# Dense expert gates: one-hot matrices and matmuls, or indirect accumulating transfers through DRAM

## The chip, the cores and the metric

The kernel runs on one core of a Trainium2 chip. The metric is the device time of one launch in microseconds, as the median of several runs. The kernel before takes 1502.28 us (three runs, 1501.57 to 1502.87).

## What is computed

Two transformer blocks on 256 tokens of width 1024, in float32. The part that the change touches is the expert layer of the first block, with 16,384 experts. Cut to what matters:

```python
q = (xb @ w_query).reshape(t, 8, 2, 128)                 # 8 heads, two half queries each
scores = einsum("thpc,hpkc->thpk", q, sub_keys)          # against 128 keys for each half
s1, i1 = top_k(scores[:, :, 0], 16);  s2, i2 = top_k(scores[:, :, 1], 16)
cand = s1[..., :, None] + s2[..., None, :]               # 256 candidates per token and head
top_s, top_pos = top_k(cand, 16)
idx = take_along_axis(i1[..., :, None] * 128 + i2[..., None, :], top_pos)
gate = softmax(top_s)
act = gelu(einsum("td,thkd->thk", xb, expert_down[idx]))
out = einsum("thk,thkd->td", gate * act, expert_up[idx])
```

So each token uses 8 x 16 experts, the gates of an expert that several heads choose add up, and all other gates are zero. The kernel computes it densely: all 16,384 hidden values of every token, times a dense gate matrix that is zero but for 128 entries per token, times all of `expert_up`.

## The kernel before

All weights stream from DRAM as 412 tiles of 128x1024 values, two to a transfer of 1 MB. SyncE issues these transfers into `raw`, two halves of two tiles (lines 286 to 292). To keep float32 precision each tile is split: ScalarE copies it to `whi` (line 331), VectorE subtracts to get `wlo` (line 344), and TensorE makes three products for each 128x128 block, high by high, low by high and high by low (lines 348 to 350), 24 matmuls a tile. `whi` and `wlo` are rings of four; a split for tile u waits until tile u - 4 is used (`w_used`), and the engines prepare three tiles ahead (`LEAD`). Order on every engine is written out by hand, with semaphores between engines.

The tiles come in stages: 20 of the first projection (`W_PROJ1`), 8 of the output, 16 of the query (`W_QUERY`), 128 of `expert_down` (`W_EXP`, the hidden tiles), 128 of `expert_up` (`W_UP`, the up projection), then the second block. In the hidden stage each tile gives 128 experts by 256 tokens, ScalarE writes their gelu to a row of `ea` (lines 1101 and 1105). In the up projection ScalarE and VectorE split each row of `ea` into `phi` and `plo` (lines 1141 and 1560), and `add_outer` adds its products to PSUM.

The selection runs on VectorE beside the first 60 hidden tiles. `top16` finds the best 16 of 32 sets of 128 scores, then of 16 sets of 256 candidates, for all heads at once; after every 8 or 4 instructions `next_tile` puts in the `wlo` of one weight tile. ScalarE takes one exponential (line 1112). VectorE compares candidate positions with a count (line 1468), GpSimd multiplies the comparison by the key numbers (line 312), VectorE sums (line 1482). TensorE transposes keys and gates (line 754).

The dense gates are built from hidden tile 64 on. For a group of four tokens VectorE writes one-hot matrices of the second key (`one_hots`, line 1492) and of the first key (line 1493), the latter times the gate in three bfloat16 parts (line 1499); TensorE multiplies them, 12 matmuls a group (`gate_group`, line 762), and VectorE multiplies the result into `ea` (`apply_gates`, line 1507). One group follows each weight tile: the 64 groups of the first half of the experts beside hidden tiles 64 to 127, those of the second half beside the first 64 tiles of the up projection.

## Time and profile before

| | |
|---|---|
| median of three runs | 1502.28 us |
| span of the profiled execution | 1499.1 us |
| TensorE busy | 1423.8 us, 95% |
| VectorE busy | 1107.4 us, 74% |
| ScalarE busy | 689.6 us, 46% |
| GpSimd busy | 25.0 us, 2% |
| moved by DMA | 223.04 MB, mean 149 GB/s |

Busy times say which engine could be the bound; matmuls are pipelined, so TensorE's busy time is no sum of costs. The chain that ended last is followed back from the end of the run and tells which instructions set the time. "L762" is line 762 of the kernel. An idle time is put down to the instruction that released it.

### The profile page before, as it was taken

Reading aid. Unit: us, or ns where it says so; the run is one execution under the profiler, and the core shown is the slowest. Engines: PE = TensorE matmul, PEld = TensorE weight load, DVE = VectorE, ACT = ScalarE, POOL = GpSimd, SP = SyncE. Lnnn points to the kernel's source line nnn. Section 1 sums busy time; section 2 is a strip of 40 time slices with the busy share of each in tenths; the row PEclk is TensorE's granted clock in tenths of the full one; section 3 lists DMA queues with packets and bytes.
Section 4 is the critical chain, followed back from the end, with each engine's and each line's share of the span. In section 5 each row is a group of like instructions: output and inputs, shape, how many; then the busy total and the mean of one; then the engine's idle time right before and its main releaser. Section 6 shows DMA issues by size and latency. Waiting matters only on the chain.

```text
span 1499.1 us, 32502 instructions
## 1 busy us (share of the span) xinstructions
PE 1423.8 (95%) x12164; PEld 1392.5 (93%) x12164; DVE 1107.4 (74%) x1975; ACT 689.6 (46%) x1012; POOL 25.0 (2%) x15
## 2 busy tenths in 40 slices
PE   6999999999699999999999999999998998999986
PEld 6998899999699999999999999999988897999986
DVE  6775737999968888888899996555576667666665
ACT  5823456667453333333333334444454444444434
POOL 0000000000500000000000000000000000000000
PEclk9999999999899999999999999999999998999998
DMA  5320344455254334443444434555554224555532
GB/s 214 127 99 1 143 169 145 166 194 181 99 197 141 140 140 140 142 146 135 143 147 148 147 140 147 189 175 189 176 194 153 101 97 157 172 195 173 193 113 85
DMA packets 31311, 223.04 MB, mean 149 GB/s; under 512 B 3553, under 2 KB 3681, under 8 KB 4497
## 3 DMA queue, kind: packets, MB, share of 16 engines
q1 hardware_dynamic: 30528, 218.22, 41.3%
q0 software_dynamic: 720, 3.97, 0.8%
q8 instruction: 42, 0.69, 0.2%
q14 instruction: 21, 0.16, 0.0%
HBM read 221.13 MB, written 1.05 MB: 148 GB/s over the span
## 4 chain that ended last, share of the span: by engine, by line
PE 82%; DVE 10%; issue 3%; ACT 3%; DMA 2%; ACTq 0%; DVEq 0%; SPq 0%
PE ps L348 24%; PE ps L349 23%; PE ps L350 23%; PE ps L762 6%; DVE wlo L344 3%; DMA raw<-in_wts 1%; ACT whi L331 1%; DVE h L491 1%; PE ps L456 1%; DVE i L1441 1%; DVE sc L1438 1%; DVE sq L428 1%; PE ps L704 0%; PE ps L623 0%; DVE alo L512 0%
## 5 line engine op out<-in xcount | busy, mean ns | idle before, releaser
L344 DVE TENSOR_TENSOR wlo<-raw,whi 128x1024 fp32r<-128x1024 f32 x412 | 502.2, 1222 | 168.8 <-ACT whi L331 164.6
L331 ACT ACTIVATE whi<-raw 128x1024 fp32r<-128x1024 f32 x412 | 435.2, 1058 | 403.9 <-PE ps L350 354.9
L348 PE MATMUL ps<-ahi,whi 128*128 128x256 f32 x2016 | 586.0, 291 | 28.3 <-DVE wlo L344 12.7
L349 PE MATMUL ps<-alo,whi 128*128 128x256 f32 x2016 | 574.0, 285 | 0.0
L350 PE MATMUL ps<-ahi,wlo 128*128 128x256 f32 x2016 | 573.5, 284 | 0.0
L348 PEld LDWEIGHTS ps<-ahi,whi 128*128 128x128 f32 x2016 | 391.4, 194 | 36.2 <-issue 27.1
L349 PEld LDWEIGHTS ps<-alo,whi 128*128 128x128 f32 x2016 | 390.6, 194 | 0.3 <-issue 0.2
L350 PEld LDWEIGHTS ps<-ahi,wlo 128*128 128x128 f32 x2016 | 390.2, 194 | 0.0
L348 PE MATMUL ps<-phi,whi 128*128 128x256 f32 x1200 | 342.7, 286 | 1.6 <-DVE plo L1560 1.6
L349 PE MATMUL ps<-plo,whi 128*128 128x256 f32 x1200 | 339.0, 282 | 0.0
L350 PE MATMUL ps<-phi,wlo 128*128 128x256 f32 x1200 | 338.3, 282 | 0.0
L348 PEld LDWEIGHTS ps<-phi,whi 128*128 128x128 f32 x1200 | 228.4, 190 | 2.2 <-DVE plo L1560 2.0
L350 PEld LDWEIGHTS ps<-phi,wlo 128*128 128x128 f32 x1200 | 225.7, 188 | 0.0
L349 PEld LDWEIGHTS ps<-plo,whi 128*128 128x128 f32 x1200 | 225.3, 188 | 0.0
L1560 DVE TENSOR_TENSOR plo<-ea,phi 128x256 fp32r<-128x256 f32 x128 | 54.5, 426 | 100.3 <-ACT phi L1141 98.0
L1105 ACT ACTIVATE ea<-ps 128x256 f32 x120 | 46.2, 385 | 175.7 <-PE ps L350 175.6
L762 PE MATMUL ps<-oh,oh 128*128 128x64 bf16 x1536 | 116.5, 241 | 0.0
L762 PEld LDWEIGHTS ps<-oh,oh 128*128 128x128 bf16 x1536 | 93.9, 119 | 5.6
L1507 DVE TENSOR_TENSOR ea<-ea,ps 128x256 f32 (+1 forms) x128 | 95.9, 750 | 0.0
L1499 DVE TENSOR_TENSOR oh<-oheq,gT 128x768 bf16<-128x768 bf16 x128 | 71.5, 559 | 14.4
L1492 DVE TENSOR_TENSOR oh<-iota,kT 128x512 bf16<-128x512 bf16 x128 | 53.6, 418 | 3.9 <-PE ps L762 3.9
L1141 ACT ACTIVATE phi<-ea 128x256 fp32r x124 | 49.6, 400 | 2.2 <-DVE ea L1507 2.2
(321 smaller groups left out, 963.0 us busy)
## 6 DMA issues: line engine op xcount, KB each, us to landing
raw<-in_wts SPq DMA_DIRECT2D x206, 1024.0 KB, 4.8
cst<-in_c POOLq DMA_DIRECT2D x1, 1216.0 KB, 12.6
x<-in_x_t SPq DMA_DIRECT2D x1, 1024.0 KB, 5.0
kk<-in_keys POOLq DMA_DIRECT2D x1, 1024.0 KB, 5.1
out_dram<-h SPq DMA_DIRECT2D x4, 256.0 KB, 2.5
cs<-in_c POOLq DMA_DIRECT2D x1, 960.0 KB, 5.1
wp<-in_w_pool POOLq DMA_DIRECT2D x1, 256.0 KB, 13.0
pt<-in_ple_t POOLq DMA_DIRECT2D x1, 256.0 KB, 5.8
```

The costliest lines, as they stand in the source:

```text
L331: nc.scalar.activation(whi[:, j, :], raw_tile(j // 2, j % 2), ACT.Copy).then_inc(s["w_hi"], 1)
L344: nc.vector.tensor_tensor(wlo[:, j, :], raw_tile(j // 2, j % 2), whi[:, j, :].bitcast(F32), ALU.subtract).then_inc(s["w_lo"], 1)
L348: nc.tensor.matmul(out_ap, wh, xh, start=first, stop=False, skip_group_check=True)
L349: nc.tensor.matmul(out_ap, wh, xl, start=False, stop=False, skip_group_check=True)
L350: return nc.tensor.matmul(out_ap, wl, xh, start=False, stop=last, skip_group_check=True)
L762: m = tm(bank(2 + j, half, base=t * half), oh2[:, j, :, t], oh1[:, j, part, :, t], start=part == 0, stop=part == 2)
L1105: A(row_of(quad * 4 + (base + n)), bank(n % 2, T), ACT.Gelu).then_inc(s["gelu"], 1)
L1141: A(phi[:, n % 2, :], row_of(quad * 4 + (base + n)), ACT.Copy).then_inc(s["p_hi"], 1)
L1492: V.tensor_tensor(oh2[:, j, :, :], iota[:, :, :], m3(v[1], P), ALU.is_equal)
L1499: V.tensor_tensor(oh1[:, j, :, :, :], oheq[:, j, :, :].unsqueeze(1).to_broadcast([P, 3, half, GT]), v.unsqueeze(2).to_broadcast([P, 3, hal ...
L1507: V.tensor_tensor(v, v, bank(2 + j, GT * half).rearrange("p (t e) -> p t e", t=GT), ALU.mult)\
L1560: V.tensor_tensor(plo[:, r, :], src, phi[:, r, :].bitcast(F32), ALU.subtract).then_inc(s["p_split"], 1)
```

## The change

The dense gates are no longer computed by matmul. A DRAM scratch `gates_dense` with one float for each expert and token (16.8 MB) is zeroed by four transfers from GpSimd's queue during the first projection. VectorE selects head by head, beginning in the query stage, and writes for each head and each of 16 choices the place of its gate in the scratch (`spot`) and the gate. `spend` counts booked microseconds and puts in a weight tile's `wlo` each 1.5. ScalarE takes the exponential of each head ahead of the hidden tiles listed in `EXP_AT`. GpSimd multiplies nothing; for each head it issues 32 indirect transfers that add 128 gates each, one per partition, to the scratch, with a wait for all earlier ones between heads. When all have landed it reads the scratch back, four tiles to a transfer, into two buffers `gd`, and in the up projection VectorE multiplies each row of `ea` by its tile of `gd`, two tiles ahead, before ScalarE makes `phi`. `gate_group`, the one-hots, the transposes of keys and gates and `apply_gates` are gone, and the up projection is one loop over 128 tiles.

```diff
+BEAT = 1.5
+EXP_AT = (0, 8, 20, 32, 44, 56, 68, 80)
...
+        dense = nc.dram_tensor("gates_dense", (N_EXP * P * T, 1), F32).ap()
...
+            blank = pf[:, :, :].rearrange("p a t -> p (a t)")
+            nc.gpsimd.memset(blank, 0.0).then_inc(s["zero_ok"], 1)
+            pl.wait_ge(s["zero_ok"], 1)
+            rows_ = dense.rearrange("(p a b) o -> p a (b o)", p=P, b=2 * T)
+            n_rows = rows_.shape[1] // 4
+            for part in range(4):
+                pl.wait_ge(s["evac"], 4 * part + 2)
+                pl.dma_start(rows_[:, part * n_rows:(part + 1) * n_rows, :], m3(blank, n_rows)).then_inc(s["zeroed"], 16)
...
-            for half_, e in ((0, eq0), (1, eq1)):
-                pl.wait_ge(s["key_eq"], half_ + 1)
-                nc.gpsimd.tensor_tensor(e[:, :, :, :], e[:, :, :, :],
-                                        i16s[:, :, half_, :].unsqueeze(2).to_broadcast([P, TB * NH, TOPK, TOPK]),
-                                        ALU.mult).then_inc(s["key_mul"], 1)
...
+            pl.wait_ge(s["zeroed"], 64)
+            for h in range(NH):
+
+                pl.wait_ge(s["pick"], h + 1)
+                if h:
+                    pl.wait_ge(s["scat"], 16 * TB * TOPK * h)
+                for tb in range(TB):
+                    for k in range(TOPK):
+                        pl.indirect_dma_start(
+                            out=dense, out_offset=bass.IndirectOffsetOnAxis(ap=spot[:, tb, h, k:k + 1], axis=0),
+                            in_=gate[:, tb, h, k:k + 1], in_offset=None, compute_op=ALU.add).then_inc(s["scat"], 16)
+            pl.wait_ge(s["scat"], 16 * TB * TOPK * NH)
+            by_tile = dense.rearrange("(n p t) o -> p n (t o)", p=P, t=T)
+            for quad in range(N_EXP // 4):
+                if quad >= 2:
+                    pl.wait_ge(s["g_mul"], 4 * (quad - 1))
+                pl.dma_start(gd[:, quad % 2, :, :], by_tile[:, 4 * quad:4 * quad + 4, :])\
+                  .then_inc((s["gd0"], s["gd1"])[quad % 2], 16)
...
-            def gate_group(j):
-                for t in range(GT):
-                    for part in range(3):
-                        m = tm(bank(2 + j, half, base=t * half), oh2[:, j, :, t], oh1[:, j, part, :, t],
-                               start=part == 0, stop=part == 2)
-                m.then_inc(s["g_ps"], 1)
...
+            with pe.Fori(0, N_EXP // 4) as i:
                 for n in range(4):
                     pe.wait_ge(s["w_lo"], i * 4 + (W_UP + n + 1))
                     pe.wait_ge(s["p_split"], i * 4 + (n + 1))
                     add_outer(n, phi[:, n % 2, :], plo[:, n % 2, :])
...
+            def p_hi(n, quad=None):
+                if quad is None:
+                    act.wait_ge(s["g_mul"], n + 1)
...
+            for h in range(NH):
+
+                act.wait_ge(s["cv_ready"], h + 1)
+                A(cv[:, h % 2, :, :], cv[:, h % 2, :, :], ACT.Exp).then_inc(s["cv_exp"], 1)
+                until = EXP_AT[h + 1] if h + 1 < NH else N_EXP - 4
+                if until > EXP_AT[h]:
+                    with act.Fori(EXP_AT[h] // 4, until // 4) as i:
+                        for n in range(4):
+                            gelu(n, i)
+            for n in range(N_EXP - 4, N_EXP):
+                gelu(n)
+                if n == N_EXP - 3:
+                    p_hi(0)
...
+            def spend(us):
+
+                spent[0] += us
+                if spent[0] >= BEAT:
+                    spent[0] -= BEAT
+                    next_tile()
...
+            def candidates(h):
+
+                dve.wait_ge(s["scores"], 2 * h + 2)
+                top16(lambda k: v16[:, k[0], k[1], :], lambda k: i16[:, k[0], k[1], :],
+                      lambda k: sc[:, k[0], 2 * h + k[1], :], [(tb, c) for tb in range(TB) for c in range(2)], 0.28)
+                ch(V.tensor_tensor(cand4, over_k(v16[:, :, 0, :]), over_j(v16[:, :, 1, :]), ALU.add))
...
+            def choose(h):
+
+                best = cv[:, h % 2, :, :]
+                top16(lambda tb: best[:, tb, :], lambda tb: ci[:, tb, :], lambda tb: cand[:, tb, :], [0, 1], 0.42)
+                ch(V.tensor_copy(gsum[:, 0, :], best[:, :, 0]))
+                V.tensor_tensor(best, best, b3(gsum[:, 0, :], TOPK), ALU.subtract).then_inc(s["cv_ready"], 1)
...
+                    ch(V.tensor_tensor(eq3, b3(cf[:, c, :, :].rearrange("p b k -> p (b k)"), TOPK),
+                                       m3(count[:, 0:TOPK], TB * TOPK), ALU.is_equal))
+                    spend(0.7)
+                    ch(V.tensor_tensor(eq[:, :, :, :], eq[:, :, :, :], over_j(i16f[:, :, c, :]), ALU.mult))
+                    spend(0.7)
+                    ch(V.tensor_reduce(out=key[:, c, :, :].rearrange("p b k -> p (b k)"), in_=eq3, op=ALU.add, axis=AX.X))
+                    spend(0.7)
+                ch(V.scalar_tensor_tensor(key[:, 0, :, :], key[:, 0, :, :], float(P), key[:, 1, :, :], ALU.mult, ALU.add))
+                V.scalar_tensor_tensor(spot[:, :, h, :], key[:, 0, :, :], float(T), b3(count[:, TOPK:], TOPK),
+                                       ALU.mult, ALU.add)
+                spend(0.3)
...
+                dve.wait_ge(s["cv_exp"], h + 1)
+                soft = cv[:, h % 2, :, :]
+                ch(V.tensor_reduce(out=gsum[:, 1, :], in_=soft, op=ALU.add, axis=AX.X))
+                ch(V.reciprocal(gsum[:, 2, :], gsum[:, 1, :]))
+                V.tensor_tensor(gate[:, :, h, :], soft, b3(gsum[:, 2, :], TOPK), ALU.mult).then_inc(s["pick"], 1)
...
+                candidates(h)
+                if h:
+                    weigh(h - 1)
+                choose(h)
+                locate(h)
+            next_tile(3)
+            weigh(NH - 1)
...
-            def apply_gates(g, t, j, h):
-
-                dve.wait_ge(s["g_ps"], g + 1)
-                v = ea[:, h * half:(h + 1) * half, :].rearrange("p e t -> p t e")
-                v = v[:, t:t + GT, :] if isinstance(t, int) else v[:, bass.ds(t, GT), :]
-                V.tensor_tensor(v, v, bank(2 + j, GT * half).rearrange("p (t e) -> p t e", t=GT), ALU.mult)\
-                 .then_inc(s["g_mul"], 1)
...
+            def apply(n, oct_=None):
+
+                got = (s["gd0"], s["gd1"])[n // 4 % 2]
+                if oct_ is None:
+                    dve.wait_ge(got, n // 8 * 16 + 16)
+                    e = n
+                else:
+                    dve.wait_ge(got, oct_ * 16 + (n // 8 * 16 + 16))
+                    e = oct_ * 8 + n
+                V.tensor_tensor(row_of(e), row_of(e), gd[:, n // 4 % 2, n % 4, :], ALU.mult).then_inc(s["g_mul"], 1)
...
+            def output_step(n, oct_=None):
+                u = W_UP + n + LEAD
+                if oct_ is not None or n + 2 < N_EXP:
+                    apply(n + 2, oct_)
+                if oct_ is not None or n + 1 < N_EXP:
+                    p_lo(n + 1, oct_)
+                split_lo(dve, None, u % 4, oct_ * 2 + u // 4) if oct_ is not None else lo_for(u - LEAD)
```

## Rows read from the trace of the kernel before

**Rows 1.** The page: busy us (share); busy tenths, 40 slices.

```profile
PE 1423.8 (95%) x12164; PEld 1392.5 (93%) x12164; DVE 1107.4 (74%) x1975; ACT 689.6 (46%) x1012; POOL 25.0 (2%) x15
...
PE   6999999999699999999999999999998998999986
```

**Rows 2.** The page: chain that ended last, shares by line.

```profile
PE ps L348 24%; PE ps L349 23%; PE ps L350 23%; PE ps L762 6%; DVE wlo L344 3%; DMA raw<-in_wts 1%; ACT whi L331 1%; DVE h L491 1%; PE ps L456 1%; DVE i L1441 1%; DVE sc L1438 1%; DVE sq L428 1%; PE ps L704 0%; PE ps L623 0%; DVE alo L512 0%
```

**Rows 3.** Stretches: us, engines' busy us (x instructions), PEclk, DMA share, GB/s.

```profile
184.40:238.30 53.90, 53.46 (x448) 53.05 (x447) 21.39 (x21) 28.40 (x50) 0.00 (x0) 1.00 0.45 156
238.30:441.40 203.10, 189.08 (x1540) 187.71 (x1539) 189.51 (x487) 128.19 (x161) 19.78 (x2) 0.97 0.46 162
441.40:678.50 237.10, 236.07 (x2318) 233.18 (x2316) 192.03 (x324) 88.38 (x131) 0.00 (x0) 1.00 0.41 145
678.50:913.40 234.90, 234.84 (x2292) 231.74 (x2292) 210.39 (x377) 87.10 (x129) 0.00 (x0) 1.00 0.41 143
913.40:1098.50 185.10, 184.58 (x1536) 184.37 (x1536) 100.08 (x128) 87.04 (x127) 1.12 (x2) 1.00 0.51 180
```

**Rows 4.** The page's groups, gates: busy, mean ns | idle before, releaser.

```profile
L762 PE MATMUL ps<-oh,oh 128*128 128x64 bf16 x1536 | 116.5, 241 | 0.0
```

**Rows 5.** Waits of TensorE, 380 to 410 us: us, times, longest.

```profile
PE ps L348 <- DVE wlo L344: 12.2, 2, 6.1
```

**Rows 6.** Timeline of VectorE: start us, us, line, operation, shape.

```profile
374.99 2.28 DVE L1468 TENSOR_TENSOR eq<-cf,iota 128x2048 f32<-128x2048 f32 x1
...
378.32 11.11 DVE L1468 TENSOR_TENSOR eq<-cf,iota 128x2048 f32<-128x2048 f32 x1
...
394.56 8.43 DVE L1477 TENSOR_TENSOR gates<-cv,gsum 128x256 f32<-128x256 f32 x1
```

**Rows 7.** Timeline of GpSimd, transfers it issues among it.

```profile
2.98 0.53 POOL L304 DMA_DIRECT2D cst<-in_c  x1
3.50 0.54 POOL L305 DMA_DIRECT2D wp<-in_w_pool  x1
155.06 0.54 POOL L307 DMA_DIRECT2D kk<-in_keys  x1 [151.03 <-DVE alo L512]
...
377.36 9.93 POOL L312 TENSOR_TENSOR eq<-eq,i16f 128x4096 f32<-128x4096 f32 x1 [221.23 <-DVE eq L1468]
392.85 9.86 POOL L312 TENSOR_TENSOR eq<-eq,i16f 128x4096 f32<-128x4096 f32 x1 [5.57 <-DVE eq L1468]
1094.87 0.58 POOL L316 DMA_DIRECT2D cs<-in_c  x1 [692.16 <-DVE plo L1560]
```

**Rows 8.** Transfers: xcount, KB each, median us to landing.

```profile
raw<-in_wts SPq DMA_DIRECT2D x206, 1024.0 KB, 4.8
...
out_dram<-h SPq DMA_DIRECT2D x4, 256.0 KB, 2.5
```

**Rows 9.** Timelines of ScalarE, then VectorE, near the up projection's end.

```profile
1092.75 1.06 ACT L331 ACTIVATE whi<-raw 128x1024 fp32r<-128x1024 f32 x1 [1.51 <-PE ps L350]
1093.71 0.40 ACT L1141 ACTIVATE phi<-ea 128x256 fp32r x1
...
1094.14 0.43 DVE L1560 TENSOR_TENSOR plo<-ea,phi 128x256 fp32r<-128x256 f32 x1 [1.32 <-ACT phi L1141]
1094.49 1.22 DVE L344 TENSOR_TENSOR wlo<-raw,whi 128x1024 fp32r<-128x1024 f32 x1
```

**Rows 10.** Timeline of VectorE in the selection.

```profile
241.79 1.64 DVE L1436 MAX8 v<-sc 128x8 f32<-128x128 f32 x8
...
252.46 1.23 DVE L344 TENSOR_TENSOR wlo<-raw,whi 128x1024 fp32r<-128x1024 f32 x1
...
255.83 1.23 DVE L344 TENSOR_TENSOR wlo<-raw,whi 128x1024 fp32r<-128x1024 f32 x1
```

**Rows 11.** Stretches of the first projection and the delta rule.

```profile
28.00:75.00 47.00, 44.97 (x361) 44.12 (x360) 35.41 (x62) 38.15 (x58) 0.00 (x0) 0.96 0.37 125
...
98.00:150.00 52.00, 46.43 (x381) 44.63 (x381) 34.27 (x50) 15.55 (x28) 0.00 (x0) 0.98 0.02 8
```

More of the change, by code:

```diff
@@ L1125, in _ @@
-            for n in range(4):
-                gelu(n, None, half)
-            with act.Fori(1, N_EXP // 8) as i:
-                for n in range(4):
-                    gelu(n, i, half)
-            def p_hi(n, quad=None, base=0):
-                u = W_UP + base + n + LEAD
-                if quad is None:
-                    if base + n >= 2:
-                        act.wait_ge(s["w_used"], W_UP + base + n - 1)
-                    A(phi[:, n % 2, :], row_of(base + n), ACT.Copy).then_inc(s["p_hi"], 1)
-                    split_hi(act, u, u % 4)
-                else:
-                    act.wait_ge(s["w_used"], quad * 4 + (W_UP + base + n - 1))
-                    A(phi[:, n % 2, :], row_of(quad * 4 + (base + n)), ACT.Copy).then_inc(s["p_hi"], 1)
-                    split_hi(act, None, u % 4, quad + u // 4)
@@ L1146, in _ @@
+            split_hi(act, W_UP + LEAD, (W_UP + LEAD) % 4)
+            for n in range(1, 4):
                 p_hi(n)
[L1147 removed]
+                split_hi(act, W_UP + n + LEAD, (W_UP + n + LEAD) % 4)
+            with act.Fori(1, N_EXP // 4) as i:
                 for n in range(4):
                     p_hi(n, i)
[L1150 to L1153 removed]
+                    split_hi(act, None, (W_UP + n + LEAD) % 4, i + (W_UP + n + LEAD) // 4)
@@ L1540, in _ @@
-            lay_out(1, None, 0)
-            def hidden_step(n, quad=None):
-                u = W_EXP + half + n + LEAD
-                split_lo(dve, None, u % 4, quad + u // 4) if quad is not None else lo_for(u - LEAD)
-                lay_out(n + 2, quad, 0) if n < half - 2 else lay_out(n + 2 - half, None, 1)
-                apply(n, quad, 0)
-            dve.wait_ge(s["gelu"], half)
-            for n in range(4):
-                hidden_step(n)
-            with dve.Fori(1, N_EXP // 8 - 1) as i:
-                for n in range(4):
-                    hidden_step(n, i)
@@ L1554, in _ @@
-            for n in range(half - 4, half):
-                hidden_step(n)
-            def p_lo(e, r):
-                dve.wait_ge(s["p_hi"], e + 1)
-                src = ea[:, e, :] if isinstance(e, int) else ea[:, bass.ds(e, 1), :].rearrange("p a t -> p (a t)")
-                V.tensor_tensor(plo[:, r, :], src, phi[:, r, :].bitcast(F32), ALU.subtract).then_inc(s["p_split"], 1)
-            def output_step(n, quad=None, h=0):
-                e = n + 1 + h * half
-                u = W_UP + h * half + n + LEAD
-                if quad is not None or n < half - 1:
-                    p_lo(e if quad is None else quad * 4 + e, (n + 1) % 2)
-                split_lo(dve, None, u % 4, quad + u // 4) if quad is not None else lo_for(u - LEAD)
-                if h == 0:
-                    if quad is not None or n < half - 2:
-                        lay_out(n + 2, quad, 1)
-                    apply(n, quad, 1)
@@ L1573, in _ @@
[L1573 to L1587 removed]
+                    lo_for(at[0])
@@ new lines, in _ @@
+            for h in range(NH):
+                candidates(h)
[5 more added lines that the diff above has]
+            weigh(NH - 1)
+            next_tile((W_EXP - at[0]) % 4)
+            assert at[0] % 4 == 0 and at[0] + 4 < W_UP, at[0]
+            with dve.Fori(at[0] // 4, W_UP // 4 - 1) as i:
+                for j in range(4):
+                    split_lo(dve, None, (j + LEAD) % 4, i + (j + LEAD) // 4)
@@ new lines, in p_lo @@
+            def p_lo(n, oct_=None):
+                if oct_ is None:
+                    dve.wait_ge(s["p_hi"], n + 1)
+                    e = n
+                else:
+                    dve.wait_ge(s["p_hi"], oct_ * 8 + (n + 1))
+                    e = oct_ * 8 + n
+                V.tensor_tensor(plo[:, n % 2, :], row_of(e), phi[:, n % 2, :].bitcast(F32), ALU.subtract)\
+                 .then_inc(s["p_split"], 1)
+            lo_for(W_UP - 4)
+            dve.wait_ge(s["gelu"], 2)
+            apply(0)
@@ L1590, in _ @@
+            with dve.Fori(0, N_EXP // 8 - 1) as i:
+                for n in range(8):
+                    output_step(n, i)
+            for n in range(N_EXP - 8, N_EXP):
+                output_step(n)
             dve.wait_ge(s["w_used"], W_V2)
-            dve.wait_ge(s["g_mul"], 2 * N_GROUPS)
             ch(V.tensor_tensor(wm[:, :], vec[:, CV["norm_mid"]:CV["norm_mid"] + KT],
```

307 lines of the change are left out of this document (83 added, 224 removed).

## The prediction

> **What bounds the kernel now.** I read the page's busy times and slices first [rows 1]. The reader is to see TensorE busy for 95% of the span, almost without a dip. The chain that ended last [rows 2] says the same by line: 70% of it are the three products of a weight tile (L348 to L350), and 6% are the matmuls of line 762, which build the dense gates. So an instruction taken off TensorE shortens the run, one taken off another engine does so only where TensorE waits for it. Then I cut the span into stages [rows 3]. A tile of weights is 24 matmuls. The last stretch there, the second half of the up projection, has 1536 matmuls and nothing else, in 185.1 us: 64 tiles at 2.89 us, TensorE never idle. That is the floor of a tile. The other three stretches also hold 64 tiles each: 203.1, 237.1 and 234.9 us. What stands above 185.1 in them is what the change can take.
>
> **What it removes.** (a) The gate groups. In the two middle stretches the matmul counts are 2318 and 2292 instead of 1536, which are 65 and 63 groups of 12 matmuls; all 1536 such matmuls are one row [rows 4]. That row's busy time is no cost, since matmuls overlap in it; the stretches give it: 237.1 - 185.1 = 52.0 and 234.9 - 185.1 = 49.8, together 101.8 us, 0.80 a group. All of it is on the path. (b) The first stretch stands 18.0 us above the floor. 12.2 us of that are TensorE waiting for VectorE's wlo [rows 5], around 387 and 402 us. The cause is in two timelines. GpSimd's multiplication of the one-hot matrices runs from 377.36 and from 392.85, 9.9 us each [rows 7], and a VectorE comparison that takes 2.28 us beforehand takes 11.11 beside it, and a 128x256 product 8.43 [rows 6]; both end when GpSimd's does, and wlo is queued behind them. The changed kernel has no such GpSimd instruction, so the 12.2 us go. The other 5.8 us are VectorE's selection running close to TensorE's pace; I let them go too and put 3 us against it below. (c) VectorE loses one-hots, gated one-hots and the product from PSUM of each group. They were beside TensorE's work and are worth nothing by themselves.
> Removed: 101.8 + 18.0 = 119.8 us.
>
> The 9.9 us rows are a lock between two engines: the Trainium skill, SBUF — State Buffer, section on who interferes with whom, says that a VectorE instruction with two SBUF inputs and a GpSimd instruction that reads SBUF exclude each other for a whole instruction. By that rule the trace agrees. An indirect transfer reads its offsets from SBUF, so the rule also speaks against this change (second rival).
>
> **What it adds beside the path.** (d) VectorE now chooses per head, from the query stage on. Eight 128-wide maxima take 1.64 us, and eight searches with one wlo 3.37 us from wlo to wlo [rows 10], of which wlo is 1.22: 0.21 and 0.27 each. A head has 8 and 12 of these, 4.9 us; the same on 256 columns 4 and 6 times, at 1.1 ns an element more (2.28 us for 2048 columns, [rows 6]), 3.9; seven passes over 512 columns at 0.7, 4.9; some fifteen small ones at 0.15, 2.2. That is 16 us. The code books 17.7 us a head and gives out a weight tile each 1.5, so a head spans 11.8 tiles, and VectorE has 1.22 + 16/11.8 = 2.6 us of work per tile against 2.89. It fits, by 10%. (e) ScalarE runs eight small exponentials in place of one, each with a change of tables; ScalarE is busy 128 of 203 us there [rows 3] and three tiles ahead. (f) In the up projection VectorE gets one 128x256 product per tile, like plo's 0.43. Per tile it is now 0.43 + 1.22 in 2.88, idle over 1 us before plo [rows 9]; the product goes into that gap. If the cover were gone it would cost 0.35 us a tile. I book 3 us for (d) to (f) together.
> (g) Zeroing writes 16.8 MB in four transfers, released while the first projection runs. That stretch moves 125 GB/s at a DMA share of 0.37, and 98 to 150 us is empty, 0.02 [rows 11]. By 125/0.37 = 338 GB/s the zeroes need 50 us of all engines; free are 0.63 x 47 + 0.98 x 52 = 81 us. They end before 150, ahead of the keys' transfer, which is queued behind them on GpSimd and starts at 155.06 [rows 7]. A weight load of 4.8 us [rows 8] may double meanwhile; four tiles of 2.89 less two copies of 1.06 and one wlo of 1.22 [rows 9] allow about 8. Cost 0 to 10 us, I take 0. (h) The reading back is 0.5 MB per four tiles. The last stretch moves 180 GB/s [rows 3]; 46 more make 226 of 338. A quad has four tiles, 11.5 us, to land; loads land in about 5 [rows 8]. Cost 0 to 6, I take 0.
>
> **The term that decides: 256 indirect transfers on GpSimd's queue.** There are 8 heads of 32, a wait for all landings between heads, and the up projection may not begin before they are all there and the first quad is read. When does a head's work arrive? The query stage runs 16 tiles in 53.9 us; the hidden tiles begin at 238.3 [rows 3]. The first head's gate comes after 24.5 us of booked work, 16 tiles, hence behind the second or third hidden tile, about 246. Each following head comes 11.8 tiles later, 34 us; the last at about 478. The up projection begins at 238.3 + 2 x 185.1 = 608.5, and ScalarE's first phi, with the products ahead of it, must be out by some 604; take 4.5 us for the first quad: the scatters must have landed by 599.5.
> With X us of GpSimd per transfer and 3.5 us of landing per head, a head takes 32X + 3.5. Above X = 0.95 that is longer than 34 us and the heads queue up: they end at 246 + 8 x (32X + 3.5) = 274 + 256X. Hidden up to X = 1.27. Each 0.1 us above costs 25.6 us, straight onto the path, since GpSimd, VectorE and ScalarE then all stand before the first product. The gain is gone at X = 1.27 + 117/256 = 1.73.
> No row shows an indirect transfer. The nearest are direct ones, 0.53 to 0.58 us each for 128 rows, which issue back to back without waiting for landings [rows 7]. That is the lower bound. The upper one is each transfer held until it lands, 2.5 us for the quickest row [rows 8]: 914, 314 us late. I take 1.1 us: near the direct row because the queue and number of rows are the same, doubled because an offset is read for each row and an accumulating element reads its target too. Then 274 + 282 = 556, 44 us early.
> The Trainium skill, DMA: Bandwidth & Descriptors, section on the anatomy of a GpSimd transfer, gives about 2.0 us fixed per transfer, mostly the receipt of the write, and its rules for kernel authors advise against many small ones. Our back-to-back rows say that this part overlaps; an estimate with 2.0 unhidden would be 274 + 512 = 786, late by 186, or 1571 us.
>
> **Sum.** 119.8 - 3 = 117 us off. The profiled execution spans 1499.1 us and the median is 1502.3, 3.2 outside the span, which I leave as it is: 1382 in the span, 1385 as median.
>
> **Rivals.** *Scatters a little late*, X from 1.27 to 1.73: at 1.5 they end at 658, 58 us late, 1443. For it: margin is only 0.17 us per instruction. *The lock.* If an indirect transfer takes VectorE's shared port for its whole 1.1 us, each two-input VectorE instruction, about 1.8 a tile, waits some 0.5 us, VectorE rises from 2.6 to 3.5 us per tile and becomes the bound: 0.6 us for some 80 tiles, 48 us, 1433. For it: [rows 6]. Against it: the transfer issued at 1094.87 took 0.58 us while wlo, from 1094.49, took its usual 1.2 [rows 7, 9], though that transfer reads no offsets. *Slower than before*: descriptors for single 4-byte elements, or their read-modify-write in DRAM, cost over 1.73 us per transfer. The place is GpSimd's queue between 246 us and the up projection; at X = 2.2 the scatters end at 837, 238 late, 1623 us. For it: 32,768 single elements have to be added one by one; against it: the engines are more than half free there (DMA share 0.41 to 0.46).
>
> **How the numbers follow.** Hidden, 1385 (1376 to 1395): 0.50. A little late, 1443: 0.14. Lock, 1433: 0.06. Slower, from 1505 up: 0.28. Near the old time by a lateness that just eats the gain: 0.02. Runs of this kernel can tell about 0.2%, 3 us. So faster 0.70, same 0.02, slower 0.28. The range begins at 1376 (no allowance, floor tiles a little better) and must reach into the slow case: beyond X = 2.0, 1571, I leave about 0.17. Range 1376 to 1575; of the likeliest case alone, 1376 to 1395.
>
> **What would show it.** Line 762 gone and four stretches of 64 tiles at about 185 us each; no VectorE instruction of 8 to 11 us; GpSimd's indirect issues near 1.1 us, 32 to a head, the last landed before about 600 us; no TensorE wait at the start of the up projection. Wrong would be: a gap there equal to 274 + 256X - 599.5; GpSimd's issues above 1.27; wlo far above 1.22 beside indirect issues; weights landing later than 8 us in the first 100 us.

## The result: 5.3% slower, and the profile after

The changed kernel takes 1581.4 us, the kernel before 1502.3: 1.053 times as long, 95% interval 1.052 to 1.055. The forecast was 1385. The page of the changed kernel, first the busy times, then slices, the chain by line, and groups (busy, mean ns | idle before, releaser):

```profile
PE 1319.3 (84%) x10622; PEld 1293.6 (82%) x10622; DVE 937.5 (59%) x1700; ACT 742.3 (47%) x1056; POOL 469.5 (30%) x306
...
PE   6989999999999995000059999999999998999986
...
POOL 1000005887888787877820000000000000000000
PEclk9999999999999998555579999999999998999998
...
POOL gates_dense L323 27%; PE ps L366 16%; PE ps L367 15%; PE ps L368 15%; DMA raw<-in_wts 2%; DMA gates_dense<-gate,spot 2%; DVE wlo L362 2%; DVE h L509 1%; ACT whi L349 1%; DVE sq L446 1%; PE ps L474 0%; DVE alo L530 0%; PE ps L722 0%; PE ps L641 0%; PE ps L630 0%
...
L323 POOL DMA_INDIRECT gates_dense<-gate,spot x256 | 434.8, 1698 | 174.0 <-issue 88.0
...
L1468 DVE TENSOR_TENSOR ea<-ea,gd 128x256 f32 (+1 forms) x128 | 53.4, 418 | 197.8 <-DMA gd<-gates_dense 197.8
```

The reader is to see the hole of zeros in TensorE's row, where before there was none [rows 1], and GpSimd half busy in the seventh slice and at seven or eight tenths from the eighth until that hole ends. TensorE is busy 104 us less in all than before, as meant. The chain names the one thing that took its place: 27% of it are the indirect transfers of line 323, and line 762 [rows 2, 4] is gone. Cut into stages (us, busy us of PE, PEld, DVE, ACT, POOL with instructions, PEclk, DMA share, GB/s): query stage, hidden tiles, hole, up projection.

```profile
187.60:241.40 53.80, 53.37 (x447) 52.95 (x446) 39.31 (x103) 28.31 (x49) 0.55 (x1) 1.00 0.45 157
241.40:615.00 373.60, 370.17 (x3069) 368.40 (x3067) 257.32 (x570) 265.52 (x330) 289.19 (x162) 1.00 0.66 177
615.00:806.40 191.40, 0.07 (x2) 0.03 (x1) 2.32 (x5) 1.86 (x4) 147.19 (x97) 0.51 0.23 6
806.40:1177.40 371.00, 370.73 (x3072) 370.36 (x3072) 243.72 (x383) 175.29 (x257) 23.55 (x32) 0.99 0.63 225
```

The up projection's 128 tiles take 371.0 us and the hidden tiles 373.6; twice the floor of [rows 3] is 370.2. So the removed 117 us did come, in the stages forecast. Between the two stands a hole of 191.4 us with 97 instructions of GpSimd in it. Take the forecast span of 1382, add 191.4 for the hole and 3.2 for the stages ahead (below), and 1576.6 stands beside the measured 1577.1.

### The profile page after: what moved, and what is told of

The parts are those of the page before. It is cut to its first block, busy times and chain, and to the rows that moved or that the text cites. A ratio compares the mean times of both kernels' runs of the same rounds, so it can differ in the third digit from the quotient of the medians.

```text
span 1577.1 us, 28668 instructions
## 1 busy us (share of the span) xinstructions
PE 1319.3 (84%) x10622; PEld 1293.6 (82%) x10622; DVE 937.5 (59%) x1700; ACT 742.3 (47%) x1056; POOL 469.5 (30%) x306
## 2 busy tenths in 40 slices
DMA packets 76939, 256.62 MB, mean 163 GB/s; under 512 B 40992, under 2 KB 41136, under 8 KB 50128
## 4 chain that ended last, share of the span: by engine, by line
PE 51%; POOL 27%; issue 8%; DVE 7%; DMA 5%; ACT 2%; SPq 0%; DVEq 0%; ACTq 0%; POOLq 0%
POOL gates_dense L323 27%; PE ps L366 16%; PE ps L367 15%; PE ps L368 15%; DMA raw<-in_wts 2%; DMA gates_dense<-gate,spot 2%; DVE wlo L362 2%; DVE h L509 1%; ACT whi L349 1%; DVE sq L446 1%; PE ps L474 0%; DVE alo L530 0%; PE ps L722 0%; PE ps L641 0%; PE ps L630 0%
## 5 line engine op out<-in xcount | busy, mean ns | idle before, releaser
L366 PE MATMUL ps<-phi,whi 128*128 128x256 f32 x1200 | 337.5, 281 | 191.6 <-DVE plo L1477 191.6
L323 POOL DMA_INDIRECT gates_dense<-gate,spot x256 | 434.8, 1698 | 174.0 <-issue 88.0
L1468 DVE TENSOR_TENSOR ea<-ea,gd 128x256 f32 (+1 forms) x128 | 53.4, 418 | 197.8 <-DMA gd<-gates_dense 197.8
L331 POOL DMA_DIRECT2D gd<-gates_dense x32 | 24.1, 753 | 326.1 <-DVE ea L1468 312.8
L1064 ACT ACT_TABLE_LOAD x31 | 39.8, 1283 | 1.7
## 6 DMA issues: line engine op xcount, KB each, us to landing
gates_dense<-pf POOLq DMA_DIRECT2D x4, 4096.0 KB, 16.8
```

The costliest lines, as they stand in the source:

```text
L323: pl.indirect_dma_start(out=dense, out_offset=bass.IndirectOffsetOnAxis(ap=spot[:, tb, h, k:k + 1], axis=0), in_=gate[:, tb, h, k:k + 1], ...
L331: pl.dma_start(gd[:, quad % 2, :, :], by_tile[:, 4 * quad:4 * quad + 4, :])\
L366: nc.tensor.matmul(out_ap, wh, xh, start=first, stop=False, skip_group_check=True)
L1064: A(row_of(quad * 4 + n), bank(n % 2, T), ACT.Gelu).then_inc(s["gelu"], 1)
L1468: V.tensor_tensor(row_of(e), row_of(e), gd[:, n // 4 % 2, n % 4, :], ALU.mult).then_inc(s["g_mul"], 1)
```

## Why the transfers take as long as they do

What GpSimd waited for ahead of its scatters (us, times, longest), and its timeline at the first four and at the last of them, with the first reading back:

```profile
POOL gates_dense L323 <- issue: 88.0, 248, 4.2
POOL gates_dense L323 <- DVE gate L1439: 64.2, 1, 64.2
...
POOL gates_dense L323 <- DMA gates_dense<-gate,spot: 21.7, 7, 4.9
```

```profile
253.37 2.61 POOL L323 DMA_INDIRECT gates_dense<-gate,spot  x1 [64.21 <-DVE gate L1439]
256.27 2.44 POOL L323 DMA_INDIRECT gates_dense<-gate,spot  x1 [0.30 <-issue]
259.02 2.47 POOL L323 DMA_INDIRECT gates_dense<-gate,spot  x1 [0.30 <-issue]
261.80 1.54 POOL L323 DMA_INDIRECT gates_dense<-gate,spot  x1 [0.30 <-issue]
...
794.50 1.54 POOL L323 DMA_INDIRECT gates_dense<-gate,spot  x1 [0.30 <-issue]
796.34 1.54 POOL L323 DMA_INDIRECT gates_dense<-gate,spot  x1 [0.30 <-issue]
799.70 0.82 POOL L331 DMA_DIRECT2D gd<-gates_dense  x1 [1.81 <-DMA gates_dense<-gate,spot]
```

The gates were waited for once, at the start; after that GpSimd always had work, so its queue is the bound from 253 us to 798. With VectorE idle ("at rest" below), a transfer takes 1.54 us and 0.30 to the next, 1.84 together. That is the cost I had taken at 1.1. The queue adds up exactly: 434.8 busy + 88.0 between + 21.7 for landings = 544.5, and 253.4 + 544.5 = 797.9. Per transfer, without landings, X = (434.8 + 88.0)/256 = 2.04.

The 434.8 us are 40.6 more than 256 x 1.54. Those 40.6 are in the longer ones, such as the first three. VectorE's timeline beside them:

```profile
253.22 1.23 DVE L362 TENSOR_TENSOR wlo<-raw,whi 128x1024 fp32r<-128x1024 f32 x1
...
256.06 1.23 DVE L362 TENSOR_TENSOR wlo<-raw,whi 128x1024 fp32r<-128x1024 f32 x1 [0.29 <-ACT whi L349]
...
258.85 1.23 DVE L362 TENSOR_TENSOR wlo<-raw,whi 128x1024 fp32r<-128x1024 f32 x1 [0.38 <-DVE cv L1385]
...
261.85 1.22 DVE L362 TENSOR_TENSOR wlo<-raw,whi 128x1024 fp32r<-128x1024 f32 x1
```

wlo had begun 0.15, 0.21 and 0.17 us before the first three transfers, which took 2.61, 2.44 and 2.47; it began 0.05 us after the fourth, which took 1.54. A transfer that finds wlo in progress ends about 1.54 us after wlo does; wlo itself keeps its 1.23. The whole trace says the same: 77 of the 256 transfers start while a wlo is in progress, and they hold 39.8 us of the lengthening; the other 179 hold 0.5 together. And 93 of the 412 wlo start while a transfer is in progress, none of them longer than 1.23 us. So the lock is there, but the other way round from my rival: GpSimd waits, VectorE does not.

My theory after the result: the time is the queue of 256 instructions, a fixed piece per instruction that consists of the indirection and the addition, plus the lock. Rivals: the price is that of the single 4-byte elements or of their read-modify-write in DRAM (then it falls with the rows, and a direct transfer pays it too); or VectorE is the bound and the queue only follows. The last is answered by the waits above: after its start GpSimd never waited for a gate.

## Experiments

**Half the transfers.** Is anything but the queue late?

```diff
-                    for k in range(TOPK):
+                    for k in range(TOPK // 2):
```

The counts that the waits compare with are halved too.

> The changed kernel with 8 of the 16 choices of each head sent to DRAM (128 transfers, not 256); the gates of the other 8 are left out. Theory (the 191 us in which TensorE stands still are nothing but GpSimd's queue of 256 transfers at 2.04 us): 16 transfers and a landing take 35 us a head, the heads' own pace, the last lands near 535, TensorE does not wait at the up projection, and the run takes 1386 to 1392 us, as forecast for the hidden case. Rival (reading back, the start of the up projection or the zeroing hold it up): the gap at the up projection stays over 50 us and the run over 1440.

Measured 1387.2 us (0.924 of before, 0.923 to 0.926), span 1383.6. TensorE has no wait at the up projection at all; the transfers:

```profile
L323 POOL DMA_INDIRECT gates_dense<-gate,spot x128 | 234.8, 1834 | 131.2 <-DVE gate L1439 65.0
```

Selection, zeroing, reading back and the products with the gates are all still in this kernel, and it runs in what I had forecast for the hidden case. Everything but the number of transfers is thereby acquitted. One part of the expectation failed: the last transfer ended at 554.6 us, not near 535. 71 of the 128 transfers start in a wlo, against 77 of 256 in the changed kernel, and the mean is 1.83 in place of 1.70. The queue still sets that end, but ahead of the up projection, where it costs nothing.

**No addition.**

```diff
-                            in_=gate[:, tb, h, k:k + 1], in_offset=None, compute_op=ALU.add)
+                            in_=gate[:, tb, h, k:k + 1], in_offset=None)
```

> The changed kernel with the same 256 indirect transfers writing and not adding (gates of an expert chosen by two heads are not summed). If the addition makes an indirect transfer dear, GpSimd's duration falls from 1.54 us at rest and the gap shrinks by 25.6 us per 0.1 us. If it is free, 1.54 us and a run of 1581 us within 5 us; only the landing between heads may be shorter than 2.4 us.

Measured 1425.9 us in a single execution, 155 less. The page's group, and then the same group at rest, 610 to 640 us:

```profile
L323 POOL DMA_INDIRECT gates_dense<-gate,spot x256 | 285.2, 1114 | 170.9 <-issue 83.2
```

```profile
L323 POOL DMA_INDIRECT gates_dense<-gate,spot x24 | 23.0, 958 | 7.3 <-issue 7.3
```

The addition is worth 1.54 - 0.96 = 0.58 us of GpSimd per transfer at rest. The idle time between two stays 0.30 (7.3 us for 24). The accumulating kernel moves 128 packets per transfer, this one 16 (28,672 fewer in 256), so it could be that packets are what costs; the next run speaks to that.

**Direct transfers.** The same number of single elements, added at fixed places.

```diff
-                        pl.indirect_dma_start(
-                            out=dense, out_offset=bass.IndirectOffsetOnAxis(ap=spot[:, tb, h, k:k + 1], axis=0),
-                            in_=gate[:, tb, h, k:k + 1], in_offset=None, compute_op=ALU.add).then_inc(s["scat"], 16)
+                        pl.dma_start(spread[:, (tb * TOPK + k) * 4, h:h + 1], gate[:, tb, h, k:k + 1],
+                                     accum_op=ALU.add, allow_slow_non_contiguous=True).then_inc(s["scat"], 16)
```

> The changed kernel with 256 direct accumulating transfers of the same 128 single elements to fixed places, no offsets read; the gates land in the wrong places. If the offsets make the cost, each takes GpSimd 0.55 to 0.7 us as the direct rows of before, all is hidden and the run takes 1386 to 1392. If single elements with an addition make it, it stays near 1.5 us and the run over 1500. The waits behind VectorE's two-input instructions should be gone, since nothing is read by GpSimd.

Measured 1388.5 us in a single execution, no wait of TensorE at the up projection. All 256 (in the trace each lasts into the next ones, up to eight at a time, so the mean is not the cost of one; busy time is):

```profile
L324 POOL DMA_DIRECT2D gates_dense<-gate x256 | 223.9, 4287 | 115.8 <-DVE gate L1439 84.1
```

223.9/256 = 0.87 us each, above the 0.55 to 0.7 expected, and this kernel moves as many packets as the changed one (76,939 both). So neither the packets nor the adding in DRAM make 1.84 us: the same elements added directly cost half of it. Nor does VectorE lengthen them: 32 in a row take 28.0 us beside the selection, and 16 at the end, with VectorE nearly idle, 14.0, the same 0.87 each. Against [rows 7], 0.53 to 0.58 for a direct transfer without adding, the addition is worth about 0.3. My two surcharges, for the offsets and for the addition, were the right two; each was too small.

**Half the rows.** 64 partitions per transfer.

```diff
-                            out=dense, out_offset=bass.IndirectOffsetOnAxis(ap=spot[:, tb, h, k:k + 1], axis=0),
-                            in_=gate[:, tb, h, k:k + 1], in_offset=None, compute_op=ALU.add).then_inc(s["scat"], 16)
+                            out=dense, out_offset=bass.IndirectOffsetOnAxis(ap=spot[0:64, tb, h, k:k + 1], axis=0),
+                            in_=gate[0:64, tb, h, k:k + 1], in_offset=None, compute_op=ALU.add).then_inc(s["scat"], 16)
```

> The changed kernel with indirect transfers of 64 rows in place of 128 (gates of 64 tokens of each block are left out). If the cost goes by the row, the duration at rest falls from 1.54 to about 0.8 to 1.0 us and the run ends at 1386 to 1450. If it is fixed for an instruction, it stays 1.54 us and the run 1581.

Measured 1546.8 us in a single execution. At rest, 650 to 750 us:

```profile
L323 POOL DMA_INDIRECT gates_dense<-gate,spot x57 | 80.4, 1410 | 22.6 <-issue 18.2 <-DMA gates_dense<-gate,spot 4.4
```

1.41 us for 64 rows, 1.54 for 128: 0.13 us for 64 rows; a straight line through both, which is an estimate from two points, leaves 1.28 fixed. Half the elements save 8% of a transfer, half the transfers save the whole excess. The rivals of the element price are out. What GpSimd does in the fixed part no run takes apart further than into the 0.58 of the addition and the rest.

**Waits by block of tokens.** A head waits only for its own block of the earlier head, not for all 32.

```diff
-                if h:
-                    pl.wait_ge(s["scat"], 16 * TB * TOPK * h)
                 for tb in range(TB):
+                    if h:
+                        pl.wait_ge(s[f"scat{tb}"], 16 * TOPK * h)
```

> The changed kernel, but a transfer of head h waits only for head h-1's transfers of its own block of 128 tokens (semaphore scat0 or scat1, one for each of the two blocks), not for all 32 of that head. Same transfers, same sums. In the changed kernel GpSimd waited 7 times, 21.7 us in all, for landings between heads. My theory (the time is GpSimd's queue of 256 transfers, and every microsecond of that queue lies on the path): the 21.7 us go, the median falls from 1581 to about 1560. Rival (the landings are needed because the accumulations pile up in the DMA engines): the transfers get longer by as much as the waits get shorter, 1575 to 1581.

Measured 1553.1 us (1.035, 1.033 to 1.036), 28 us less, where 21.7 had been expected. GpSimd has no wait for a landing left, its idle time of unknown cause is 9.1 us less, and TensorE's wait is 30.9 less than the 191.3 of the changed kernel:

```profile
L323 POOL DMA_INDIRECT gates_dense<-gate,spot x256 | 434.3, 1697 | 143.1 <-issue 78.9
```

```profile
PE ps L367 <- DVE plo L1478: 160.4, 1, 160.4
```

434.3 busy as before: the accumulations do not pile up behind GpSimd. The queue's microseconds reach the end one for one.

**One operand in wlo.** This tests the lock.

```diff
-            nc.vector.tensor_tensor(wlo[:, j, :], raw_tile(j // 2, j % 2), whi[:, j, :].bitcast(F32),
-                                    ALU.subtract).then_inc(s["w_lo"], 1)
+            nc.vector.tensor_scalar(wlo[:, j, :], raw_tile(j // 2, j % 2), 2.0 ** -13, None,
+                                    ALU.mult).then_inc(s["w_lo"], 1)
```

> The changed kernel with one instruction of VectorE exchanged: wlo is raw times 2^-13 (one SBUF operand, tensor_scalar) in place of raw minus whi (two operands). That leaves out the low part of the weights' split, so the product is less exact; the matmuls, transfers and waits are the same in number. It tests the lock. If a transfer on GpSimd has to wait for the two-operand instruction of VectorE in progress at its start, transfers beside the selection should now take their 1.54 us at rest for the most part (mean 1.54 to 1.60 in place of 1.70), the queue shortens by 25 to 40 us and the time is 1540 to 1557. Rival (the longer transfers come from VectorE's or the DMA engines' load in general, whatever the operands): mean stays 1.70, time 1575 to 1583.

Measured 1543.9 us (1.028, 1.026 to 1.030), 37 less:

```profile
L323 POOL DMA_INDIRECT gates_dense<-gate,spot x256 | 411.4, 1607 | 172.0 <-issue 87.3
```

23.4 of the 40.6 us of lengthening go with this exchange, and TensorE waits 164.5 in place of 191.3. The mean over all is 1.61, just above what I expected. wlo is also shorter now (about 0.7 us in place of 1.22), so this run alone can't tell its length from its operand. Nor is the new wlo free of the lock. About 17 us of lengthening stay, nearly all beside it: 8.0 us in the 39 transfers that start in a wlo and 8.3 in the 97 during which one begins, 0.6 in the other 120. Between 566 and 578 us VectorE runs nothing but wlo, and two transfers there take 1.73 and 1.70. Some wlo are now held themselves (1.02 us at 574.90, in place of 0.69).

The operand is told from the length in a kernel of the next section, the eight-head version that measured 1419.8. Its plain transfers take 0.96 us at rest. GpSimd's timeline, then VectorE's:

```profile
502.72 2.96 POOL L325 DMA_INDIRECT gates_dense<-gate,spot  x1 [0.30 <-issue]
505.98 0.96 POOL L325 DMA_INDIRECT gates_dense<-gate,spot  x1 [0.30 <-issue]
507.24 0.96 POOL L325 DMA_INDIRECT gates_dense<-gate,spot  x1 [0.30 <-issue]
508.51 0.95 POOL L325 DMA_INDIRECT gates_dense<-gate,spot  x1 [0.30 <-issue]
...
501.49 3.35 DVE L1467 TENSOR_TENSOR sc<-sc 128x3072 f32<-128x3072 f32 x1
...
506.02 3.34 DVE L1469 TENSOR_REDUCE gate<-sc 128x32 f32<-128x3072 f32 x1
```

The product with two inputs and the sum with one last equally long. The transfer that starts in the product takes 2.96 us; the two that start in the sum take 0.96 and 0.95.

Of the 37 us 27 are the shorter wait; the other 10 lie outside it, some 7 of them after the up projection has begun, in a kernel whose VectorE has a lighter load everywhere, and were not followed up.

**The kernel before, without its GpSimd arithmetic.** My step (b) by itself.

```diff
-                nc.gpsimd.tensor_tensor(e[:, :, :, :], e[:, :, :, :],
+                V.tensor_tensor(e[:, :, :, :], e[:, :, :, :],
```

The two multiplications also change place in VectorE's order: each comes behind its comparison and one wlo, with the next two wlo behind it.

> The kernel before, with one edit: the two multiplications of the one-hot matrices (TENSOR_TENSOR of 9.9 us each on GpSimd) are issued on VectorE, each behind its comparison, so that GpSimd and VectorE never work on these large arrays together. My step (b) (a lock between the engines makes the comparison 11.1 us in place of 2.3 and holds wlo back, TensorE waits 12.2 us): the comparison is 2.3 us, the multiplication about 2.3 on VectorE, TensorE's wait for wlo falls to 0 to 4 us, the median from 1502 to 1490 to 1495. Rival (VectorE simply has too much selection work there, and 4.6 us more on it make it worse): a wait of 12 to 17 us stays, 1502 to 1507.

Measured 1492.4 us (0.993, 0.992 to 0.995), 10 us less. VectorE's timeline at the place of [rows 6]:

```profile
377.96 4.42 DVE L1470 TENSOR_TENSOR eq<-eq,i16f 128x4096 f32<-128x4096 f32 x1
382.30 2.35 DVE L339 TENSOR_TENSOR wlo<-raw,whi 128x1024 fp32r<-128x1024 f32 x2
384.57 2.29 DVE L1463 TENSOR_TENSOR eq<-cf,iota 128x2048 f32<-128x2048 f32 x1
```

The comparison is 2.29 us instead of 11.11, and TensorE's wait for wlo in this kernel is 3.1 in place of 12.2 [rows 5]. The multiplication takes 4.4 us on VectorE, twice what I had written, and it is still the better place: 4.4 us there against 9.9 on GpSimd with VectorE held for most of it.

**Twice the zeroing**, on the kernel with half the transfers: a second scratch is zeroed beside the first.

```diff
                 pl.dma_start(rows_[:, part * n_rows:(part + 1) * n_rows, :], m3(blank, n_rows)).then_inc(s["zeroed"], 16)
+                pl.dma_start(rows2[:, part * n_rows:(part + 1) * n_rows, :], m3(blank, n_rows)).then_inc(s["zeroed"], 16)
```

> The kernel of the run with half the choices (8 of 16 a head, so the sums of gates are incomplete; 1387.2 us, no wait at the up projection), with twice the zeroing: a second scratch of the same 16.8 MB is zeroed beside the first and never read. In the changed kernel the stages ahead of the hidden tiles took 3.2 us longer than before, which I put down to the zeroing. If that is so and the price is by the byte, this adds another 3 to 10 us: 1390 to 1397. Rival (those 3.2 us are the first head's selection work among the query tiles, the zeroing is free): 1387 to 1388.

Measured 1392.4 us against 1387.2 for the kernel that it is made from (0.927 of before, 0.926 to 0.929, against 0.923 to 0.926). The first projection's stretch in the changed kernel and the same in this one:

```profile
28.00:75.00 47.00, 43.70 (x350) 42.86 (x349) 34.78 (x61) 35.51 (x54) 3.73 (x3) 0.96 0.96 364
```

```profile
28.00:75.00 47.00, 41.07 (x320) 40.37 (x320) 31.97 (x56) 32.58 (x50) 6.92 (x6) 0.93 0.97 372
```

Before, TensorE got through 361 matmuls there [rows 11], now 350, and 320 with twice the zeroes. The engines of the transfers are full (DMA share 0.96), and the weights come late for a few tiles. The last copy of the query stage starts at 237.8 us before, 241.0 in the changed kernel, 241.3 in the one with half the transfers and 247.0 here. The first 3.2 us are there before the query stage begins (184.4 us before [rows 3], 187.6 in the changed kernel), and VectorE's selection begins only in that stage, so the rival is out. A zeroing of 16.8 MB costs 3 to 6 us.

## A version that is faster than both

The runs say what would help: no addition and no wait for landings, with the sum kept. A write without adding is right if it carries the whole sum. So VectorE compares the 16 expert numbers of a head with those of all earlier heads of the token, multiplies matches by their gates, reduces, and adds the result to the head's own gate; where two heads chose the same expert, the later write replaces the earlier one with the sum of both. First for six of eight heads (h is the head, J = 16h):

```diff
+                ch(V.tensor_tensor(same, eid(h, h + 1).unsqueeze(3).to_broadcast(shape),
+                                   eid(0, h).unsqueeze(2).to_broadcast(shape), ALU.is_equal))
+                ch(V.tensor_tensor(same, same, raw(0, h).unsqueeze(2).to_broadcast(shape), ALU.mult))
+                ch(V.tensor_reduce(out=gate[:, :, h, :], in_=same, op=ALU.add, axis=AX.X))
+                V.tensor_tensor(gate[:, :, h, :], gate[:, :, h, :], raw(h, h + 1), ALU.add).then_inc(s["pick"], 1)
```

> A version drawn from the runs, which computes the whole result. Heads 0 to 5 are written without adding: VectorE compares a head's 16 expert numbers with those of all earlier heads of the token (is_equal, multiplication by their gates, reduction), adds what matches to the head's own gate, and a later write to the same element simply replaces the earlier one. Heads 6 and 7 add as before. The waits are one semaphore for each block of tokens. By my account the addition costs 0.58 us of the queue for each of 192 transfers, 111 us; the landings 20 us; the new two-input instructions of VectorE (15 units of 2 x 0.54 us) hold transfers up by 5 to 16 us. Expected 1455 to 1470, against 1502 before and 1581 changed. Rival (VectorE becomes the bound with about 24 us more of work among the hidden tiles, and the transfers wait for the gates): 1475 to 1500, with TensorE waiting for wlo.

Measured 1445.6 us (0.964, 0.960 to 0.968), 9 below the range expected; TensorE waits 52.2 at the up projection. The work on VectorE found room: TensorE stays full in the hidden stage. Then all eight heads, with VectorE's pace raised:

```diff
-BEAT = 1.5
-MERGED = 6
-EXP_AT = (0, 8, 20, 36, 52, 68, 84, 96)
+BEAT = 1.7
+MERGED = 8
+EXP_AT = (0, 8, 20, 32, 44, 60, 76, 92)
```

> The version of the run before (expert numbers compared on VectorE, later writes replace earlier ones), now for all eight heads, so that no transfer adds; VectorE is given 1.7 us of booked selection work per weight tile in place of 1.5, which brings the last head's gates to about tile 103, 540 us, and ScalarE's exponentials stand at tiles 0, 8, 20, 32, 44, 60, 76 and 92. The run with six heads merged measured 1445.6. By my account 64 more transfers lose 0.58 us each, 37 us, and the longer comparisons (two two-input instructions of 3.3 and 3.8 us for the last two heads) give back 5 to 10: 1412 to 1422. Rival (VectorE is now over TensorE's 2.88 us per tile and delays the hidden tiles): 1425 to 1445, with TensorE waiting for wlo before 600 us.

Measured 1594 us (1.059), its four executions from 1582 to 1613: neither theory. The trace is that of the longest, 1612.5 us. In it TensorE stands still inside tiles, for nothing that the profile shows:

```profile
288.45 0.58 PE L371 MATMUL ps<-alo,whi 128*128 128x256 f32 x1 [1.03 <-issue]
289.18 0.57 PE L372 MATMUL ps<-ahi,wlo 128*128 128x256 f32 x1 [0.15 <-issue]
291.97 0.37 PE L370 MATMUL ps<-ahi,whi 128*128 128x256 f32 x1 [2.22 <-issue]
```

TensorE is not alone in this: from 241 to 600 us ScalarE stands 143.7 us for no instruction of this core, and VectorE 143.7 us for ScalarE's whi. So VectorE is not over its pace there. Two runs to tell the pace from the eight heads. Eight heads at a pace of 1.6, with the exponentials moved to match:

> All eight heads merged, as in the run that measured 1594, with the pace between the two (1.6 us of selection booked per weight tile; exponentials at tiles 0, 8, 20, 32, 48, 64, 80, 96). In that run TensorE stood still inside single tiles of the hidden stage, 2 to 11 us at a time, for nothing that the profile shows, from the first tiles on (246 to 300 us), although the six-head version has the same instructions there. If the pace of 1.7 or something of that one run was the cause, this is 1412 to 1425, the price of 64 additions (37 us) less than 1445.6. If eight merged heads as such bring the stalls (rival), it is 1550 or more, with TensorE idle inside tiles again.

Measured 1419.8 us (0.945, 0.944 to 0.947), as expected. Six heads at the pace of 1.7:

> Six heads merged, as in the run of 1445.6, with the pace of the run of 1594 (1.7 us of selection booked per weight tile; exponentials at tiles 0, 8, 20, 32, 44, 60, 76, 84). If the pace brings the stalls inside tiles, 1550 or more. If not (my theory: the queue alone sets the time, and the gates arrive earlier than it needs them), 1438 to 1448, as before.

Measured 1443.4 us (0.961, 0.958 to 0.964), as expected too. So neither the eight heads nor the pace alone brings the stalls. What did so in that one kernel stays open: the two together, or something outside the program in those executions.

The eight-head version is the fastest one here that computes the whole result. Its transfers:

```profile
L325 POOL DMA_INDIRECT gates_dense<-gate,spot x256 | 302.7, 1183 | 143.1 <-issue 81.3
```

(302.7 + 81.3)/256 = 1.50 us, the last from 637.3 to 638.3, TensorE's wait 20.7. The transfer at rest is 0.96 + 0.30 = 1.26; at that rate 256 of them would have ended at 577, ahead of the 599.5 of my forecast, but the last head's gates come only at 560.9, and its 32 transfers from there would end at 601. So without the lock it would be hidden to within some 3 us (an estimate, with 1.7 for the landing). The lock is the rest: 58.5 us of lengthening, 37.7 of it in transfers that start in a wlo and 17.7 in those that start in one of the new two-input comparisons and products, which last up to 3.9 us.

## Why the prediction was wrong, step by step

- **The term that decides, X.** This is the step that failed, by its size alone. I took 1.1 us by doubling the nearest row; measured is 2.04: 1.54 busy at rest, 0.16 by the lock (40.6/256), 0.34 between two. The formula around it held: 274 + 256 x 2.04 = 796 against 797.9 measured, late by 197 against a hole of 191. The start was 253.4 where I had 246, the landings 21.7 where I had 28, and these two cancel. The "doubling for an offset and a read of the target" had no row behind it. From [rows 7] to the measured 1.84 at rest it is a factor of 3.3. In parts: 0.55 for a direct transfer; 0.71 more for an indirect one without adding (0.96 + 0.30 against 0.55); and 0.58 more for adding 128 elements, where a direct transfer pays 0.3.
- **The range** ended at 1575, and its far case was given 0.28. Its threshold, 1.73 us, had been worked out, and 1.84 at rest is past it by a tenth of a microsecond. A term that decides by 256 times its error, and whose bounds were 0.53 and 2.5, did not bear 0.50 for X below 1.27, nor 0.70 for faster.
- **Slower, the rival,** had the right place and nearly the right price (2.2, 1623) but the wrong mechanism: element size and read-modify-write. The runs with direct transfers and with 64 rows exclude it as the whole price; that is for the most part fixed work of GpSimd per indirect instruction, of which the addition is 0.58. This is also where an estimate from the Trainium skill stood: DMA: Bandwidth & Descriptors, section on the anatomy of a GpSimd transfer, with 2.0 us fixed gave 1571, near the 1581 measured. By that section the fixed part is mostly the receipt of the write, and that is not what fills this queue: in the kernel without any wait for landings the transfers were as long as ever (434.3 us), and direct ones follow each other at 0.87. The receipt is seen once by itself, behind the last transfer, where GpSimd waits 1.81 us more. The number was near, for another reason.
- **(a), (f), the floor.** Right: 371.0 and 373.6 us for 128 tiles where the floor is 370.2. **(d), (e)** came to 3.4 us together in the hidden stage, 3 booked.
- **(b)** Right, and shown by the kernel before without GpSimd's arithmetic: 10 us of the 12.2. One reading was loose: the comparison does not end with GpSimd's multiplication (387.3 us) but at 389.4, 2.1 us later, so it was held until then and ran afterwards [rows 6, 7].
- **When the gates arrive.** The last head's were ready at 489.6 us, not 478. With the queue behind, that changed nothing.
- **The lock as a rival.** I priced it as VectorE's loss, 48 us; it is GpSimd's, 40.6 us of the queue, and VectorE loses nothing. The argument against it, a direct transfer of 0.58 us beside wlo, was about another kind of instruction, as I had noted. By the rule of the Trainium skill, SBUF — State Buffer, section on who interferes with whom, whichever starts first holds the other off for its whole instruction. The trace agrees for wlo before a transfer, and not for the reverse: wlo begun 0.05 us after a transfer took its usual 1.22, and so did the 92 others begun during one.
- **(g)** Zeroing: 3.2 us, and 5 to 6 for the second one; inside the 0 to 10, not the 0 that I took. One sign of being wrong came true: a weight load issued at 66.7 us took 9.4 to land, over the 8 that the buffers allow. **(h)** Reading back: nothing found, in the kernel where nothing else is late.

## What to carry to other kernels

Count the instructions on GpSimd's queue before the bytes: a term of the form "so many instructions times an unknown" should be carried to its threshold first, and if the threshold lies within the bounds, the sign is open, however good the rest of the sum is. Don't price an indirect transfer from a direct one. When work is moved off the bounding engine onto an idle one, ask for that engine's throughput over the whole stretch, here 346 us for 256 instructions, rather than for its being idle. And an accumulating scatter can be made a plain one if the collisions are summed beforehand on an engine with room.

## What the runs showed of the hardware

- An indirect transfer of 128 single elements occupies GpSimd 1.54 us with adding and 0.96 without, and 0.30 us pass before the next; 64 elements take 1.41. Direct adding ones follow each other at 0.87.
- An indirect transfer that starts while VectorE's two-operand wlo runs is longer by about what is left of it (2.61 in place of 1.54 us); a one-input sum of 3.34 us lengthens none. Of VectorE's wlo that begin during a transfer (93 in the changed kernel) none is longer. Between GpSimd's and VectorE's arithmetic in the kernel before it was VectorE that waited, 8 to 9 us at a time [rows 6].
- With TensorE idle from 615 us on, the granted clock was 0.51 over the hole, its lower level (1.2 GHz), and it was still there at the start of the up projection: the first 18 matmuls start 0.21 us apart, until 810.16 us, the later ones 0.12. That costs about 1.7 us; the whole stage took 371.0 us against 370.2.
